# Turning an expert's further rows ahead of the former expert's further down products, in a mixture-of-experts decoder layer

## What is computed

```python
def body(acc, blk):
    rows, rw, e = blk
    xb = x_pad[rows]
    h = jax.nn.silu(xb @ w_gate[e]) * (xb @ w_up[e])
    yb = (h @ w_down[e]) * rw[:, None].astype(xb.dtype)
    return acc.at[rows].add(yb), None
```

## Time and profile before

| | us |
|---|---|
| median of 3 runs | 1648.62 |
| the profiled execution, its own time | 1649.76 |
| its span, first to last instruction | 1648.1 |
| PE busy | 1581.8 (96%) |
| VectorE busy | 1188.4 (72%) |
| ScalarE busy | 1031.4 (63%) |
| GpSimd busy | 515.5 (31%) |

### The profile page before, as it was taken

The page is one execution under the profiler, slowest core; times in us unless marked ns, Lnnn a source line. Parts: engine busy times, 40 slices in busy tenths (PEclk is TensorE's granted clock), DMA queues, the critical chain, the costliest instruction groups (busy, mean ns, idle before and its releaser), DMA issues.

```text
span 1648.1 us, 32180 instructions
## 1 busy us (share of the span) xinstructions
PE 1581.8 (96%) x8246; PEld 1313.5 (80%) x8247; DVE 1188.4 (72%) x2036; ACT 1031.4 (63%) x1705; POOL 515.5 (31%) x495
## 2 busy tenths in 40 slices
PE   6999999999999999899999999999999999999985
PEld 6897888888887788778888888788888888888863
DVE  4214777777777887846777787767876787888857
ACT  3214666666666654526677787666776777877854
POOL 0000000000000134532554464543454454454526
PEclk9999999999999999899999999999999999999995
DMA  7223322222223534557999999999999999999986
GB/s 244 90 81 90 72 52 64 59 63 70 52 64 113 177 116 160 202 190 277 329 300 319 300 357 367 329 288 267 336 316 284 280 354 324 347 368 365 375 258 250
DMA packets 161319, 368.63 MB, mean 224 GB/s; under 512 B 53008, under 2 KB 73488, under 8 KB 161264
## 3 DMA queue, kind: packets, MB, share of 16 engines
q1 hardware_dynamic: 136272, 284.21, 49.4%
q0 software_dynamic: 24992, 83.73, 19.7%
HBM read 294.39 MB, written 65.11 MB: 218 GB/s over the span
## 4 chain that ended last, share of the span: by engine, by line
PE 72%; DVE 7%; issue 7%; DMA 5%; ACT 4%; ACTq 1%; POOL 1%; another core or an unknown queue 1%; POOLq 1%; DVEq 1%; SPq 0%
PE bank L1023 6%; PE bank L1026 6%; PE bank L1029 6%; DMA sums_scratch<-ys,sidx 4%; PE q_ps L91 4%; PE q_ps L93 4%; PE q_ps L92 4%; PE out_ps L914 4%; PE k_ps L893 3%; PE out_ps L1082 3%; PE out_ps L1083 3%; PE q_ps L1013 3%; PE k_ps L1050 2%; PE k_ps L1051 2%; PE k_ps L1058 2%
## 5 line engine op out<-in xcount | busy, mean ns | idle before, releaser
L1915 DVE TENSOR_TENSOR gu_lo<-raw_gu,gu_hi 128x1024 fp32r<-128x1024 f32 x260 | 306.4, 1220 | 25.7 <-ACT gu_hi L1394 23.3
L1394 ACT CAST gu_hi<-raw_gu 128x1024 fp32r<-128x1024 f32 x260 | 253.3, 1050 | 1.2 <-DMA raw_gu<-in_moe_w_up_dram 1.2
L1023 PE MATMUL bank<-gu_hi,xb_hi 128*128 128x512 f32 x576 | 234.5, 407 | 6.3 <-DVE gu_lo L1915 3.2
L1026 PE MATMUL bank<-gu_lo,xb_hi 128*128 128x512 f32 x576 | 228.1, 396 | 0.0
L681 POOL DMA_INDIRECT sums_scratch<-ys,sidx x63 | 124.3, 1973 | 144.7 <-DMA sums_scratch<-ys,sidx 108.7
L1915 DVE TENSOR_TENSOR dn_lo<-raw_dn,dn_hi 128x1024 fp32r<-128x1024 f32 x130 | 152.7, 1213 | 2.4 <-ACT dn_hi L1394 1.8
L1029 PE MATMUL bank<-gu_hi,xb_lo 128*128 128x512 f32 x576 | 142.5, 389 | 0.0
L1023 PEld LDWEIGHTS bank<-gu_hi,xb_hi 128*128 128x128 f32 x576 | 110.9, 193 | 29.9 <-issue 7.3
L612 POOL IOTA e<- 128x64 f32 x1 | 0.2, 185 | 429.0 <-DVE xs L1711 429.0
L1299 ACT CAST pt_hi<-k_ps 128x512 fp32r<-128x512 f32 (+1 forms) x192 | 85.8, 482 | 75.4 <-PE k_ps L893 74.7
L1394 ACT CAST dn_hi<-raw_dn 128x1024 fp32r<-128x1024 f32 x130 | 130.0, 1052 | 2.3 <-DMA raw_dn<-in_moe_w_down_dram 2.3
(11 more groups left out here) (305 smaller groups left out, 3991.5 us busy)
## 6 DMA issues: line engine op xcount, KB each, us to landing
raw_gu<-in_moe_w_gate_dram SPq DMA_DIRECT2D x128, 512.0 KB
raw_gu<-in_moe_w_up_dram SPq DMA_DIRECT2D x128, 512.0 KB
raw_dn<-in_moe_w_down_dram SPq DMA_DIRECT2D x128, 512.0 KB
wqk<-in_fox_w_in_dram SPq DMA_DIRECT2D x66, 128.0 KB, 2.5
v_scratch<-v_out SPq DMA_DIRECT2D x32, 256.0 KB, 2.8
va<-v_scratch SPq DMA_DIRECT2D x16, 512.0 KB, 4.8
fin<-sums_scratch SPq DMA_DIRECT2D x16, 512.0 KB, 9.6
xs<-in_x_dram SPq DMA_DIRECT2D x8, 512.0 KB, 8.3
```

The source lines that it names most:

```text
L1023: i = pe.matmul(o3, xb_hi[s][:, c], g_hi[:, :, c], start=c == 0, stop=False, skip_group_check=True)
L1026: pe.matmul(o3, xb_hi[s][:, c], g_lo[:, :, c], start=False, stop=False, skip_group_check=True)
L1394: a.copy(hi, raw).then_inc(S[done], 1)
L1915: dve.tensor_tensor(lo, raw, hi, ALU.subtract).then_inc(S[lo_ok], 1)
```

## The change

`turn_further` for expert e moves up in the case `before_it > 0`: it stands behind `turn_next` and in front of `down_further`. In the case `before_it < 1` it stays where it was in the order (behind `turn_next`, in front of `down`), but is now inside that case's body. Each of the two bodies has a branch on `nx > 0` around it. In the loop for several further blocks, a block is turned at the end of the round before its own. No product, transpose, semaphore or buffer is added or removed; no other engine's code changes.

```diff
                     pe.wait_ge(S["ht_lo_ok"], m)
                     turn_h_further(xi - 1)
                     turn_next()
+                    with pe.If(nx > 0):
+                        turn_further(par, xi)
                     down_further(par, e + 1, xi - 1)
                 with pe.If(before_it < 1):
                     turn_h(m - 1)
                     pe.wait_ge(S["g_lo_ok"], G_PIECES * (e + 2))
                     gate_up(par, w, "rows_", m + 1)
                     turn_next()
+                    with pe.If(nx > 0):
+                        pe.wait_ge(S["ht_lo_ok"], m)
+                        turn_further(par, xi)
                 with pe.If(nx > 0):
                     with pe.If(nx > 1):
                         with pe.Fori(0, nx - 1) as k:
-                            pe.wait_ge(S["ht_lo_ok"], m)
-                            turn_further(par, xi + k)
                             gate_up_further(w, xi + k)
                             turn_h_further(xi + k)
                             down_further(w, e + 2, xi + k)
-                    pe.wait_ge(S["ht_lo_ok"], m)
-                    turn_further(par, xi + nx - 1)
+                            turn_further(par, xi + k + 1)
                     down(m - 1, par, e + 1)
                     if last:
                         pe.wait_ge(S["x_rows_lo_ok"], xi + nx)
```

## The result

Over 20 runs each, the changed kernel took 1652.01 us (median; 1646.75 to 1654.47) and the kernel before 1647.32. The ratio is 1.0026, 95% interval [1.0018, 1.0033]: **slower by 4.3 us** by the ratio, and by 4.7 us from median to median. The forecast was 5.0 us slower, in the likeliest case, and a median of 1653.6 us.

What follows compares the result with a forecast made beforehand. PE's own stream was taken to bound the routed experts' stretch. A new wait of 0.33 us in each of 15 experts, the order's 0.01 gain included, gave 5.0 us: 1648.6 + 5.0 = 1653.6 us, range 1648.3 to 1657.5.

Steps and rivals of the forecast that it cites:

- What bounds the kernel, and where: Routed experts' stretch: PE's own stream, busy 798.8 of 810 us, sets the time; only 15 experts change, only gaps move.
- The order itself: Turns moved ahead of the down group in 15 experts: 16.56 us each without a wait against 16.57, worth 0.01 us.
- The "faster" rival: The 0.36 us idle PE before the turns goes and the chain is met: 5.4 us won, 1643.2 us; chance 0.05.
- The wait that is made: PE's weight load at line 1082 comes 0.41 us late, waiting for DVE: 0.33 us per expert, 5.0 us over 15.
- the cover of 2.74 us: PE's stretch from line 1101's last product start to the next weight load in former experts, against a 3.09 us chain.
- the 0.07: Line 1082's late load: the expert's period was to grow by 0.07 us less than the load is late, so 0.34.
- The level: Whole kernel: forecast median 1653.6 us, from the earlier median of 1648.62 plus 5.0, slower by 0.30%.
- The branch: Added compare and branch for each of 64 experts: hidden by the sequencer's 2.2 us lead, costing nothing; 9.1 us without it.
- The first rival: At line 1082's load: chain 0.4 us shorter or down products longer, load on time, 1648.5 us, no change; chance 0.14.
- What hangs on the wait, and what is pulled forward: Later work on PE, DVE, ACT, POOL, SP is covered; turns about 2 us earlier keep 10 us to the gather: free.

## Why the prediction was right

*What bounds the kernel, and where.* Right: 15 experts changed, the others kept their times, and only gaps moved.

*The order itself.* Forecast as worth 0.01 us, and right. The idle 0.36 us before the turns did go, and nothing came of it. The rows of the same expert before, beside those of after above, tell why:

```profile
1068.25 1.16 PE L1013 MATMUL q_ps<-ident,x_rows 128*128 128x128 f32 x8
1069.16 0.48 PE L1100 MATMUL out_ps<-dn_hi,ho 128*128 128x512 f32 x1
...
1072.52 0.39 PE L1051 MATMUL k_ps<-dn_lo,ht_hi 128*128 128x512 f32 x1
...
1075.04 0.39 PE L1082 MATMUL out_ps<-gu_hi,xo 128*128 128x512 f32 x1
```

From the start of line 1013 to the first product of line 1051 it is 1072.52 - 1068.25 = 4.27 us before and 1067.95 - 1063.68 = 4.27 after. The first rows' down products win 0.20 us, as they stand behind other products and not behind narrow transposes (0.23 + 0.23 us for their first two steps, where it was 0.32 before the turns and 0.34 behind their first product). But what follows line 1013 starts later, the turns 1.09 us behind it where the down products came 0.91 behind it, and the rest is rounding. The "faster" rival fell on this: it needed the 0.36 us as a gain and a chain that is met, and had neither.

*The wait that is made.* Right in place and cause. The load was forecast to come 0.41 us late. From the last product of line 1101 to it, the trace of after has 1070.64 - 1067.49 = 3.15 us, where the forecast had 3.09 + 0.06; and the cover of 2.74 us is that of the former experts, which did not change. The weak step was the last one, from the load's lateness to the expert's length. Forecast was 0.41 - 0.07 - 0.01 = 0.33 us after the earlier trace rows; measured is 16.87 - 16.57 = 0.30. The term that was too small is the 0.07. From the load of line 1082 to the next expert it is 1078.68 - 1074.81 = 3.87 us before and 1074.41 - 1070.64 = 3.77 after, so 0.10 is given back: behind the wait the first product starts with its load, where it started 0.23 us behind it (1075.04 against 1074.81), and the second one follows 0.34 us later. 15 x 0.30 = 4.5 us; 4.3 was measured.

*The level.* The forecast median of 1653.6 us lay 1.6 above the measured 1652.01. 1.3 of that is the base: the median of three runs before was 1648.62, that of twenty 1647.32. The upper end of the range, 1657.5, lies 8.9 us above the base, which is 1.8 times the loss reckoned and not above twice.

*The branch.* Forecast as hidden. Borne out by the run with the branches alone, 1.0001, and by the neither experts' 9.35 us. The Trainium skill's 108 ns for a compare and branch (Advanced Engine Details and Errata, Control Flow Timing) was read as 6.9 us if in the open; none of it showed. The rows of this case have 0.07 us for a branch that falls through and 0.20 to 0.21 for one that jumps, on either side of that figure.

*The first rival* (no wait) fell on the 15 new waits. It named the right quantity: 0.4 us less chain, or more cover, and the loss is gone. The run with `xo` first took the chain's last link, the making of `xo`, out of it and did just that.

*What hangs on the wait, and what is pulled forward.* Forecast as covered, and right as far as seen. The both experts differ by no more than 0.01 us whatever follows, so nothing was handed on, and line 1072 shows no wait for the gather. The 5.99 us of growth in the experts' stretch of the profiled execution are more than 4.5. The rest lies in the neither experts near the end, above all in the one before the last expert (10.94 us before, 12.77 after). PE waits 2.24 us at its end for DVE, and DVE for ACT, which waits for the weights:

```profile
1574.65 1.99 ACT L1396 CAST gu_hi<-raw_gu 128x1024 fp32r<-128x1024 f32 x2 [1.86 <-DMA raw_gu<-in_moe_w_up_dram]
```

This differs from execution to execution and not with the order: the same expert takes 11.27 us in the profile of the kernel before with the memset, and 14.45 in that of the run with the branches alone.

## What to carry to other kernels

A step that looks like mere order may be the cover of a chain on other engines. Before it is moved, measure the chain from the instruction that starts it to the one that waits, and the stream that lies between, in the new order; a stretch of the same trace that lacks the step gives the second number directly. An engine that shows idle time *before* its part of the chain is not overloaded. Its part still counts, as the 0.48 us more on DVE did, but the order in which it takes its work can take a link out of the chain for nothing. Small transposes are worth putting next to other small ones, in different groups of 32 partitions: here that was 0.33 us an expert, and another 0.21.

## What the runs showed of the hardware that was not expected

PE ran two groups of 32-row transposes at the same time when they read different groups of 32 partitions (starts 0.01 us apart), and one behind the other, 0.26 us apart, when they read the same. It was worth 0.21 us for each expert, and was seen in 8 of 15 experts, and after the rows had been moved to other partitions in all. The Trainium skill (TensorE: Matmul & The Clock Gate, Part 3: Packing small matmuls) says that a weight load overlaps products in flight only where their groups of rows differ. The trace agrees in that only differing groups ran together. It does not bear out the word "only" for the loads themselves: in the expert above whose groups were the same, the second load of line 1091 starts at 1085.25, behind the start of the first product of the same rows at 1085.15 and ahead of the next at 1085.29. I had reckoned only with the change between full and narrow transposes that is saved.
